# Down projections by seven block products in place of eight, in a two-block transformer kernel

## What is computed

```python
ff = (silu(hn @ w_gate) * (hn @ w_up)) @ w_down      # 1024x1024, 1024x2816, 2816x1024
h = h + rms_norm(ff, ffn_post_g)                     # block 1
x = x + (silu(gate) * up) @ w_down                   # block 2, then a last rms_norm
```

## Time and profile before

| | before |
|---|---|
| median of 3 runs | 2549.6 us (2549.29 to 2553.57) |
| profiled execution | 2554.41 us, its span 2552.6 us |
| TensorE (PE) busy | 2423.1 us, 95% of the span |
| weight loads (PEld) | 2018.8 us, 79% |
| VectorE (DVE) | 1160.2 us, 45% |
| ScalarE (ACT) | 895.3 us, 35% |
| GpSimd (POOL) | 987.5 us, 39% |
| mean granted TensorE clock | 0.978 of full speed |
| DMA | 212.35 MB, 83 GB/s in the mean |

### The profile page before, as it was taken

How to read it: one execution, slowest core, us unless ns; L and a number is a source line. 1 busy time by engine, 2 the same in 40 slices (tenths; PEclk the granted TensorE clock), 3 DMA queues, 4 the chain that set the end, 5 groups by cost and what they waited for, 6 DMA issues and landing times. The chain is left out here.

```text
span 2552.6 us, 29796 instructions
## 1 busy us (share of the span) xinstructions
PE 2423.1 (95%) x11766; PEld 2018.8 (79%) x11766; DVE 1160.2 (45%) x1747; ACT 895.3 (35%) x1725; POOL 987.5 (39%) x799
## 2 busy tenths in 40 slices
PE   7996889899999999999989989999989999999998
PEld 5885878688888888888988667787778888888887
DVE  4899632933233252353660666242493323325233
ACT  4124443532322232234632545223353232233122
POOL 4000103687777631232112121122068777763221
PEclk9997989999999999999999999999999999999999
DMA  4221113232322353243001000132133232225313
GB/s 144 51 55 58 59 36 117 80 116 68 98 83 88 102 194 111 74 133 89 18 17 48 26 5 17 42 135 71 54 103 116 69 97 83 90 100 195 111 58 116
DMA packets 185125, 212.35 MB, mean 83 GB/s; under 512 B 13655, under 2 KB 141368, under 8 KB 184986
## 3 DMA queue, kind: packets, MB, share of 16 engines
q1 hardware_dynamic: 174346, 172.30, 22.2%
q10 hardware_dynamic: 10640, 38.15, 3.8%
HBM read 167.00 MB, written 43.38 MB: 82 GB/s over the span
## 5 line engine op out<-in xcount | busy, mean ns | idle before, releaser
L382 POOL TENSOR_TENSOR wl<-stage,wh 128x1024 fp32r<-128x1024 f32 (+3 forms) x95 | 228.5, 2409 | 643.7 <-ACT wh L376 643.6
L410 PE MATMUL P<-wh,ah 128*128 128x512 f32 (+2 forms) x1216 | 461.3, 379 | 3.1 <-POOL wl L382 3.1
L412 PE MATMUL P<-wh,al 128*128 128x512 f32 (+2 forms) x1216 | 459.6, 378 | 0.0
L411 PE MATMUL P<-wl,ah 128*128 128x512 f32 (+2 forms) x1216 | 459.3, 378 | 0.0
L410 PE MATMUL P<-ah,wh 128*128 128x512 f32 x1120 | 439.9, 393 | 7.1 <-DVE al L440 7.1
L412 PE MATMUL P<-ah,wl 128*128 128x512 f32 x1120 | 437.8, 391 | 0.0
L411 PE MATMUL P<-al,wh 128*128 128x512 f32 x1120 | 437.7, 391 | 0.0
L410 PEld LDWEIGHTS P<-wh,ah 128*128 128x128 f32 x1216 | 230.4, 190 | 43.4 <-POOL wl L382 3.3
L412 PEld LDWEIGHTS P<-wh,al 128*128 128x128 f32 x1216 | 230.3, 189 | 40.7
L411 PEld LDWEIGHTS P<-wl,ah 128*128 128x128 f32 x1216 | 230.2, 189 | 39.7
L410 PEld LDWEIGHTS P<-ah,wh 128*128 128x128 f32 x1120 | 211.5, 189 | 52.5 <-DVE al L440 5.5
(11 more groups left out here) (304 smaller groups left out, 3885.3 us busy)
## 6 DMA issues: line engine op xcount, KB each, us to landing
raw<-ff_rows SPq DMA_DIRECT2D x52, 512.0 KB, 6.3
stage<-in_w_down_dram SPq DMA_DIRECT2D x88, 256.0 KB, 3.4
stage<-in_w_gu_dram SPq DMA_DIRECT2D x44, 512.0 KB, 5.1
ff_rows<-uo ACTq DMA_DIRECT2D x40, 512.0 KB, 3.4
h<-ht ACTq DMA_DIRECT2D x32, 512.0 KB, 4.5
xr<-h SPq DMA_DIRECT2D x32, 512.0 KB, 4.7
stage<-in_w_in_dram SPq DMA_DIRECT2D x22, 512.0 KB, 3.8
stage<-in_w_gate_dram SPq DMA_DIRECT2D x22, 512.0 KB, 4.1
```

Of the source, the lines that this page charges most:

```text
L382: port.e.tensor_tensor(WL[n % RING][:, 0:w], stage[place(n)][:, 0:w], WH[n % RING][:, 0:w].bitcast(F32), ALU.subtract).then_inc(*sig.up(n))
L410: e.matmul(out, lh, rh, start=start, stop=False, skip_group_check=onto)
L411: e.matmul(out, lh, rl, start=False, stop=False, skip_group_check=onto)
L412: return e.matmul(out, ll, rh, start=False, stop=stop, skip_group_check=onto)
```

## The change

The down projection's product is split into 2x2 blocks: tokens 0 to 511 and 512 to 1023, hidden features 0 to 1407 and 1408 to 2815, output columns 0 to 511 and 512 to 1023. Seven block products are formed in the order A11 and S1 in turn, S2 and S3 in turn, A12 and A22 in turn, then S4, 11 units each (`DOWN`, 77 units). A unit is one 128-feature step of one product: 4 token tiles x 3 matmuls. In each pair one product uses PSUM banks 0 to 3 and the other banks 4 to 7.

- **Row sums.** Behind each pair of m, VectorE makes four sums of the hidden tiles (S1, S3, S2, S4) into a new tile `SB` (`row_sums`). `put` stores seven 512-wide blocks per pair instead of four, two units later in ScalarE's order, with three DMAs.
- **Rows.** All rows of all 77 units are loaded from DRAM, 128x512 each, into 12 buffers `RF`.
- **Weights.** 47 pieces of one or two 128x512 blocks go through three `stage` buffers. VectorE makes the weight sums T1, T2, T3, T4 (`weight_sum`). T2 is also stored to DRAM by ScalarE and loaded again beside the A22 blocks.
- **Halves.** ScalarE makes the high halves of rows and weights (`down_upper`), VectorE all low halves (`down_lower`). GpSimd does no low halves in this stage. The first four units' halves are made between the sums of the last m.
- **Combining.** ScalarE copies A11 and S1 out of PSUM, and VectorE adds the other products on (24 additions of 128x512, and 4 more at the end) into eight tiles `CR`.
- **End.** Tokens 512 to 1023 (tiles 4 to 7) are complete before product S4 and tiles 0 to 3 after it, so `DownPass` takes the tiles in the order 4, 5, 6, 7, 0, 1, 2, 3. S4's last six steps run tile by tile. In block 1 the transposes of tiles 4, 5, 6, 7 and 0 stand within the S4 tail, and the next stage begins with the second half of the tokens.

The core of the diff:

```diff
+KEPT = {"A11": 0, "A12": 1, "A22": 2, "S1": 3, "S2": 4, "S3": 5, "S4": 6}
+DOWN = [(op, p) for two in (("A11", "S1"), ("S2", "S3"), ("A12", "A22"), ("S4",)) for p in range(HF) for op in two]
+TAIL = 5
+ORDER = (4, 5, 6, 7, 0, 1, 2, 3)
...
+            for i in range(1, 5):
+                AC.wait_ge(ev, (self.name, p, f"S{i}"))
+            for i, (at, src) in enumerate(((0, UO[0][:, 0:512]), (512, UO[1][:, :]),
+                                           (1536, SB[:, :, :].rearrange("p a b -> p (a b)")))):
+                AC.e.dma_start(ff_dram[p][:, at:at + src.shape[1]], src).then_inc(*l_ff[p % 2].up((self.name, p, i)))
...
+            self.row_sums(0)
             for m in range(2, NF):
-                for op in ("S2", "S3", "S1", "A22", "S4"):
+                for i, op in enumerate(("S2", "S3", "S1", "A22", "S4")):
                     self.sums(m, op)
+                    if m == self.last and i < 4:
+                        self.down_lower(i)
+                if m % 2:
+                    self.row_sums(m // 2)
+            self.down_dve()
...
+        def row_sums(self, p):
...
+            DV.wait_ge(ev, (self.name, m, "F12"))
+            e.tensor_tensor(SB[:, 0, :], f12, f22, ALU.add).then_inc(*ev.up((self.name, p, "S1")))
+            e.tensor_tensor(SB[:, 2, :], f11, f12, ALU.subtract).then_inc(*ev.up((self.name, p, "S3")))
...
+            e.tensor_tensor(SB[:, 1, :], SB[:, 0, :], f11, ALU.subtract).then_inc(*ev.up((self.name, p, "S2")))
...
+            e.tensor_tensor(SB[:, 3, :], f21, SB[:, 1, :], ALU.subtract).then_inc(*ev.up((self.name, p, "S4")))
...
+        def load_row(self, u):
...
+            if before is not None:
+                SP.wait_ge(al, (self.name, "split", before))
+            elif b >= 4:
+                SP.wait_ge(mm, (self.name, (self.last, "A22")))
...
+        def down_upper(self, u):
...
+            AC.wait_ge(l_raw[b], (self.name, u))
...
+            AC.e.activation(self.rows_place(u)[0], RF[b][:, :], ACT.Copy).then_inc(*ah.up((self.name, "split", u)))
+            ring_free(AC, ("down", self.name, u))
...
+            AC.e.activation(self.weight_place(u)[0], self.weight_whole(u), ACT.Copy).then_inc(
+                *wh.up((self.name, "d", u)))
...
+        def down_lower(self, u):
+
+            self.weight_sum(u + 1)
+            hi, lo = self.rows_place(u)
+            DV.wait_ge(ah, (self.name, "split", u))
+            DV.e.tensor_tensor(lo, RF[self.row_buffer(u)[0]][:, :], hi.bitcast(F32), ALU.subtract).then_inc(
+                *al.up((self.name, "split", u)))
+            hi, lo, _ = self.weight_place(u)
+            DV.wait_ge(wh, (self.name, "d", u))
+            DV.e.tensor_tensor(lo, self.weight_whole(u), hi.bitcast(F32), ALU.subtract).then_inc(
+                *wd.up((self.name, "d", u)))
...
+        def down_pe(self):
...
+            for u, (op, p) in enumerate(DOWN):
+                if op == "S4" and p == TAIL:
+                    break
+                for j in range(4):
+                    ins = self.down_product(u, j)
...
+            turn()
+            for j in range(4):
+                for p in range(TAIL, HF):
+                    ins = self.down_product(DOWN_AT["S4", p], j)
+                ins.then_inc(*mm.up((name, "S4", j)))
+                turn()
...
+            turn(4, (4, 5))
+            end(0)
+            end(1)
+            turn(5, (6, 7))
+            ps.residual_dve(0)
+            end(2)
+            turn(6, (4, 5))
+            ps.residual_dve(1)
+            ps.norm_dve(0)
+            end(3)
+            turn(7, (6, 7))
+            ps.residual_dve(2)
+            ps.norm_dve(1)
+            ps.residual_dve(3)
+            ps.norm_dve(2)
+            turn(0, (4, 5))
+            ps.norm_dve(3)
```

More of the change, by code:

```diff
@@ L130, in tokens, with down, block, blocks @@
                 rows(w, order[i:i + 2], [(512 * j, 512 * j + 512)])
+    def down(w):
+        def block(k, j):
+            return w[128 * k:128 * k + 128, 512 * j:512 * j + 512]
+        def blocks(srcs):
+            for i in range(0, len(srcs), 2):
+                two = srcs[i:i + 2]
+                plan.append((512 * len(two), [(lambda s, at=512 * x: s[:, at:at + 512], src)
+                                              for x, src in enumerate(two)]))
+        for k in range(HF):
+            plan.append((1024, [(lambda s: s[:, :], w[128 * k:128 * k + 128, :])]))
+        blocks([block(*b) for k in range(HF) for b in ((HF + k, 1), (k, 1), (k, 0))])
+        blocks([b for k in range(HF) for b in (block(HF + k, 0), t2[k])])
+        blocks([block(HF + k, 1) for k in range(HF)])
+        plan.extend([(0, [])] * 2)
     def ffn(name, wg, g0, wu, u0, wd):
@@ L323, in build @@
     for n in range(len(plan)):
[L324 to L329, removed]
+        (name, i), (down_name, j) = in_sevens(n), in_downs(n)
+        if plan[n][1]:
+            slot_before[n] = slot_user.get(place(n))
+            slot_user[place(n)] = n
+        if name is None and down_name is None:
+            halves = [((None, n), [2 * (n % RING), 2 * (n % RING) + 1])]
+        elif name and i == 0:
             halves = [((name, u), [(2 * (n % RING) + u) % (2 * RING)]) for u in range(len(UNITS))]
+        elif down_name and j == 0:
+            halves = [(("down", down_name, u), [(2 * (sevens[down_name] % RING) + 5 + u) % (2 * RING)])
+                      for u in range(len(DOWN))]
         else:
@@ L494, in build @@
         in_rows = 5
+        order = tuple(range(NT))
+        halves = (0, 1)
+        last_turns = ((5, (1, 2)), (6, (4, 5)), (7, (6, 7)))
         def __init__(self, name, number, old, g_post, g_pre, new, began):
@@ L1777, in load_raw @@
-        def load_raw(self, at):
-            f, b, before = self.source(at)[0], *self.raw_buffer(at)
+            SP.wait_ge(tp, ((self.turned.name, NT - 1), 4))
+            for u in range(4):
+                self.load_row(u)
+            for u in range(len(DOWN)):
+                load_to(D + self.piece_of(u))
+                if u >= 4:
+                    self.load_row(u)
+                if u == 68:
+                    self.ps.start_loads()
+            load_to(D + DOWN_PIECES + 1)
+            for i in range(NT):
+                if i + 2 < NT:
+                    self.ps.load(ORDER[i + 2])
+                if self.ps.new is None and i:
+                    self.ps.store(ORDER[i - 1])
@@ new lines, in act, with turn @@
+            ps = self.ps
+            ps.sums_act(4)
+            ps.sums_act(5)
+            self.down_upper(len(DOWN) - 1)
+            ps.squares_act(4)
+            ps.sums_act(6)
+            ps.squares_act(5)
+            send_to(self.down + DOWN_PIECES)
+            ps.sums_act(7)
+            ps.squares_act(6)
+            ps.squares_act(7)
+            send_to(self.down + DOWN_PIECES + 1)
+            turns = iter(((4, (4, 5)), (5, (6, 7)), (6, (4, 5)), (7, (6, 7)), (0, (4, 5))))
+            def turn():
+                if ps.new is not None:
+                    ps.turn_act(*next(turns))
@@ new lines, in piece_block, with weight_whole @@
+        def piece_block(self, i, j):
+            return stage[place(self.down + i)][:, 512 * j:512 * j + 512]
+        def weight_whole(self, u):
+            op, p = DOWN[u]
+            if op == "A11":
+                return self.piece_block(p, 0)
+            if op == "A12":
+                return self.piece_block(28 + p, 0)
+            if op == "S4":
+                return self.piece_block(39 + p // 2, p % 2)
+            return T2W[p % 2][:, :] if op == "S2" else self.weight_place(u)[2]
@@ L3022, in xq_dve @@
     def xq_dve():
-        for turn in LAST_TURNS:
+        for turn in wo_pass.last_turns:
             wo_pass.turn_dve(*turn)
```

507 lines of the change are left out of this document (347 added, 160 removed).

## The result

The changed kernel took **2515.7 us** in the median of 4 runs (2511.8 to 2519.5), against 2549.6 for the kernel before. The ratio is 0.9863, its 95% interval 0.9846 to 0.9881: 33.9 us faster, where 42.3 were forecast. The number lies inside the range (2497 to 2526) but 8.4 us above the predicted point and outside the band of 2502 to 2512 that had half of the chances. Two later sets of runs gave the ratios 0.9876 and 0.9873.

A forecast was written before the change was run, and what follows sets the result against it. TensorE, busy 95% of the span, was taken as the bound. Terms -59.8 + 11.2 + 3.0 + 3.3 = -42.3 us gave 2507.3 us against the median of 2549.6; range 2497 to 2526, with 2502 to 2512 given chance 0.50.

The forecast's parts named there:

- Matmuls removed: Both feed-forwards' down stages: 1056 matmuls become 924 in each, at 0.2267 us each, -59.8 us in all.
- The others can feed it: Down stages: VectorE, ScalarE and DMA keep TensorE supplied, VectorE busy 138 of 209.5 us, DMA 220 GB/s; cost 0.
- The rival of late pieces: Down stages: weight pieces or halves come late, 2527 to 2537 us, or 2515 and on with one feed-forward alone; chance 0.20.
- The rival in which VectorE becomes the bound: Down stages: VectorE's operations at contended 1.24 us, about 2612 us; it decides from 0.97 us per operation; chance 0.04.
- The first row sums: Third m, both blocks: four sums at 1.24 us delay A12; 3.9 us gap plus 1.7 for the clock, +11.2 us in all.
- the rival of locked row sums: Third m: each row sum waits out a GpSimd operation, 1.9 us; gap 6.6 us, 5.4 us more, 2513 us; chance 0.12.
- The end of block 1: Block 1's end and the next stage's start: short TensorE waits on VectorE's queue, +3.0 us, bounds 0 and 8.
- the only new wait of PE over 1.5 us stands at A12: Sign to look for: TensorE's one such new wait is at the third m, 3.9 us, in both blocks.
- the three gaps named: End of block 1: TensorE waits 0.9 us before turn(6), 1.1 before turn(0), 1.0 before the next stage's first product.
- These gaps are too short for the clock: End of block 1: waits of about 1 us there would not lower TensorE's clock, so no further cost.
- The end of block 2: Behind the last matmul: the last norm ends 8.1 us later where it was 4.8; +3.3 us, bounds 2 and 5.
- The twin of the 2.77 us gap: Stage after block 1: the existing gap before the second product group has a counterpart of about 2.4 us.

The follow-up runs named there:

- the late kernels: Changed kernel with the third m's first row sums moved behind a later addition: all four 2504.9 us (ratio 0.9815 to the kernel before), or two of them 2503.0 us.
- The experiment with the turn first: Changed kernel, but at the end of block 1 ScalarE makes a transposed tile's high half before it takes sums and squares: 2514.3 us, one execution.

## Why the prediction was nearly right, and where it was not

- **Matmuls removed, -59.8.** Right: -29.93 in block 2's down stage, at the forecast pace, and 132 matmuls fewer in block 1's too.
- **The others can feed it, 0.** Right: no product waited for an operand in either stage, nor at its start, lows took 0.68 us where 0.61 was assumed, and VectorE was busy for 152 us in 209 (138 forecast). DMA moved 51.5 MB in block 2's stage, 247 GB/s where 220 was forecast; the working left out the residual's rows and the output, 13 transfers of 512 KB. The two experiments that pressed on the stage (GpSimd's cuts, two buffers) brought no wait of a product either. The rival of late pieces, 0.20, had no part in it, though its 2515 for one feed-forward is the nearest of the forecast numbers to the 2515.7 measured: by the number alone that rival would look right, and only the traces rule it out. The rival in which VectorE becomes the bound was far from its point of 0.97 us per operation.
- **The first row sums, +11.2.** The mechanism, the place and the waiter were as stated; the late kernels show it by taking it away. The term was mis-sized: it is +14.5, 7.25 in each block (in block 1 a gap of 5.3, 1.8 for the clock behind it, and 0.16 because the gap is counted from the modelled end of a matmul). A row sum took 1.65 us, not 1.24, so the gap was 5.3 and not 3.9; the clock behind it cost 1.8 us (0.59 for 4.4 us) where 1.7 was forecast. (Added up exactly, the text's gaps of 3.9, 5.3 and 6.6 are 3.8, 5.2 and 6.5.) The step that failed is the choice of the median. The median 1.236 of the earlier trace rows covers the whole kernel, with a minimum of 0.692 in it; the row just before the place, 1.59 in the earlier trace rows, was the nearer one, and the text had kept it as a bound. The same median stood there as the evidence against the rival of locked row sums. That rival's numbers, 1.9 us and a gap of 6.6, did not come either: 5.3 lies at the bound that the 1.59 gave. The SBUF page of the Trainium skill ("SBUF — State Buffer", section "SBUF: two separate sides") has VectorE's operation with two SBUF inputs and GpSimd's shut each other out for a whole instruction. The trace agrees in kind more than the text on record allowed: one for one here, and none of it for additions that read PSUM. In size two whole operations would be 1.28 + 0.61 = 1.9 us, and 1.65 is measured.
- **The end of block 1, +3.0.** Too small by 4.8 us, the largest error, and the sign "the only new wait of PE over 1.5 us stands at A12" did not hold. Of the three gaps named, 0.9, 1.1 and 1.0, the trace has 1.13, 1.36 and 3.02 at other places. The 7.8 us are these 5.5, then 1.6 for the clock (0.64 for 4.4 us behind the longest, its slow transposes of 1.94 us included), 0.2 for slower transposes elsewhere, and 3 x 0.16 = 0.5 because a gap is counted from the end of a matmul, 0.39 us behind its start, while the next could have started 0.23 us behind it. Two steps failed. One is the working of the chain on VectorE's queue, which gave gaps of about 1 us: its operations did run at the pace of lone ones, as assumed (1.28 us for a norm), but the waits between them were left out, 2.80 us for the load of tile 6's row behind a weight chunk on SyncE's queue, 0.92 for GpSimd's root and twice 1.1 for ScalarE's turn. The experiment with the turn first shows that ScalarE's order made 1.9 us of the gap of 3.02. The late load stands in the chain ahead of the other two gaps, and where it was later still (two stage buffers) they grew; taken away alone it gave nothing, because the operation behind it then ran into GpSimd's 2.4 us cut and took 3.3 us. What it costs by itself is not shown. The other step is "These gaps are too short for the clock". It held behind the gaps of 1.13 and 1.36 us, but one gap was three times as long as forecast. As a bound it rested on one gap of 1.99 us, and the trace of before already had one of 2.00 us with the clock at 0.69 behind it. The upper bound of 8 holds the 7.8, narrowly.
- **The end of block 2, +3.3.** Right: +3.2, and 8.1 us behind the last matmul as forecast. That VectorE's chain counts in it is shown by the 0.95 us that one moved operation gave, a little less than its 1.2; 2.4 of the 8.1 us are ScalarE's squares and GpSimd's root ahead of the last norm.
- **The sum.** -42.3, + 3.3 and + 4.8 for the two terms and - 0.1 elsewhere give -34.3, and the medians moved by -33.9. The spans of the profiled executions moved by -38.7, with 4.4 us of scatter in them.

The twin of the 2.77 us gap was forecast at 2.4 and is 2.77. What sets it was not tried.

## What to carry to other kernels

Taking an eighth of the matmuls out of a stage that TensorE bounds pays in full as long as the operands' lead covers the new work; here the losses were all at the seams, where a handful of new operations was queued ahead of one short operation that TensorE awaited. Place new work on a queue behind what the bound engine needs next. In one block it gave back 11.9 of the 14.5 us that the traces show, and in pairs all of them; with two smaller moves of order the kernel came to 49.5 us below the one before, where the changed kernel beside it stood at 32.6. Measure such a cost between two instructions that both kernels share, because the gap alone missed a part of it here (3.71 us, where 7.25 were lost). And price an operation by the row next to its place, not by the median of its line, when another engine's activity changes its duration.

## What was not expected of the hardware

- Within one m, VectorE operations of one form and size took 0.77 to 1.78 us beside a busy GpSimd. With 1024 columns, one that started 0.15 us behind a GpSimd operation of 2.40 us took 3.32 and ended 1.07 us behind that one's end (1101.84 against 1100.77). Alone it takes 1.28, so it lost 2.04 us to an operation of which 2.25 were left. Moving cuts from VectorE to GpSimd left VectorE busier with 76 operations fewer (144.2 to 154.6 us).
- The granted clock fell to 0.59, 0.64 and 0.68 of full in the 4 us behind gaps of 5.32, 3.02 and 3.71 us, that is, at 1.2 GHz for most of each stretch and 2.4 for the rest. Shorter gaps went either way: 0.69 behind 1.78 and, in another execution, 2.00 us, and 1.00 behind 1.14, 1.99, 2.00 and even 2.78. The length of a gap alone does not say what follows it, and what else does was not tried.
- DMA carried 246 to 255 GB/s at a share of 0.71 to 0.74 through 200 us. Loads of 256 KB landed in 3.7 us (weights, 3.5 before) and 5.4 us (rows) in the median.
